# Reordering the hand-over between a layer norm and the next projection in an fp32 transformer kernel

## The reference

```python
def hybrid_layer(x, ...):
    proj = einsum('bsd,de->bse', x, w_in)        # 1024 -> 4864 columns
    ...                                          # pooling, window attention, gated conv
    mix = einsum('bsd,de->bse', merged, w_o)
    x = layer_norm(ALPHA * x + mix, ln1_g, ln1_b)
    up = causal_dwconv(einsum('bsd,df->bsf', x, w_up), ffn_conv_w)
    a, b = split(up, 2)
    ffn = einsum('bsf,fd->bsd', silu(a) * b, w_down)
    return layer_norm(ALPHA * x + ffn, ln2_g, ln2_b)
```

## Time and profile before

| what | value |
|---|---|
| time, median of 3 runs | 2985.54 us (2983.82 to 2987.83) |
| time of the profiled execution | 2989.49 us |
| its span, first to last instruction | 2987.5 us |
| mean granted TensorE clock | 0.994 of full speed |
| busy: PE / ACT / DVE / POOL | 2912.5 / 1591.6 / 1060.3 / 411.8 us |

### The profile page before, as it was taken

One profiled execution on the slowest core, in us unless ns is written; L12 is line 12 of the kernel. 1 busy time (PEld: TensorE's weight loads), 2 busy tenths in 40 slices (PEclk: granted clock), 3 DMA queues, 4 the chain that ended last, 5 costly groups with the idle time before them and its releaser, 6 DMA issues.

```text
span 2987.5 us, 35252 instructions
## 1 busy us (share of the span) xinstructions
PE 2912.5 (97%) x13262; PEld 2376.9 (80%) x13262; DVE 1060.3 (35%) x2146; ACT 1591.6 (53%) x2305; POOL 411.8 (14%) x477
## 2 busy tenths in 40 slices
PE   8999999999999999999998999999999899999997
PEld 6889888888887568888887887888877788788885
DVE  4534436321123764121226114422253611632234
ACT  6655656554445755444455445545554544554455
POOL 1111111111111001111110111111111011111111
PEclk9999999999999999999999999999999999999998
DMA  8676767688987328888883887787877299788876
GB/s 240 147 149 136 161 138 154 144 198 194 194 191 169 71 43 188 196 193 194 195 192 70 188 192 168 183 197 192 191 167 171 58 201 193 156 195 191 201 184 158
DMA packets 138148, 503.65 MB, mean 169 GB/s; under 512 B 15472, under 2 KB 15728, under 8 KB 137872
## 3 DMA queue, kind: packets, MB, share of 16 engines
q0 software_dynamic: 68016, 248.22, 47.2%
q1 hardware_dynamic: 69120, 251.69, 27.7%
q10 hardware_dynamic: 864, 1.72, 0.2%
HBM read 499.46 MB, written 2.10 MB: 168 GB/s over the span
## 4 chain that ended last, share of the span: by engine, by line
PE 91%; DVE 3%; ACT 2%; issue 2%; DMA 1%; DVEq 1%; ACTq 0%; POOLq 0%; POOL 0%; SPq 0%
PE ps L971 74%; PE ps L989 5%; PE ps L1342 3%; PE ps L1063 1%; DMA wl<-weights 1%; PE ps L1120 1%; PE ps L1264 1%; PE ps L1283 1%; PE ps L1265 1%; DVE arena L2086 1%; PE ps L1103 0%; PE ps L1209 0%; ACT wl L430 0%; PE ps L1272 0%; PE ps L1234 0%
## 5 line engine op out<-in xcount | busy, mean ns | idle before, releaser
L426 ACT ACTIVATE wh<-raw 128x1024 fp32r<-128x1024 f32 (+1 forms) x470 | 495.0, 1053 | 1079.8 <-PE ps L971 999.8
L971 PE MATMUL ps<-HH,wh 128*128 128x512 f32 x2304 | 905.8, 393 | 13.6 <-DVE HL L1975 5.7
L971 PE MATMUL ps<-HH,wl 128*128 128x512 f32 x2304 | 897.7, 390 | 0.0
L971 PE MATMUL ps<-HL,wh 128*128 128x512 f32 x2304 | 897.6, 390 | 0.0
L410 POOL DMA_DIRECT2D wl<-weights x470 | 409.9, 872 | 2570.7 <-ACT wl L430 2566.0
L971 PEld LDWEIGHTS ps<-HH,wh 128*128 128x128 f32 x2304 | 433.3, 188 | 110.8 <-issue 21.8
L971 PEld LDWEIGHTS ps<-HL,wh 128*128 128x128 f32 x2304 | 433.4, 188 | 91.8 <-issue 3.1
L971 PEld LDWEIGHTS ps<-HH,wl 128*128 128x128 f32 x2304 | 433.1, 188 | 90.8
L430 ACT ACTIVATE wl<-raw 128x1024 fp32r<-128x1024 f32 (+1 forms) x470 | 488.4, 1039 | 0.0
L971 PE MATMUL ps<-MH,wh 128*128 128x512 f32 x1056 | 411.9, 390 | 1.8 <-issue 0.8
L971 PE MATMUL ps<-MH,wl 128*128 128x512 f32 x1056 | 410.9, 389 | 0.0
(11 more groups left out here) (277 smaller groups left out, 2756.4 us busy)
## 6 DMA issues: line engine op xcount, KB each, us to landing
raw<-weights SPq DMA_DIRECT2D x472, 512.0 KB, 5.4
wl<-weights POOLq DMA_DIRECT2D x470, 512.0 KB, 7.8
XT<-x SPq DMA_DIRECT2D x4, 512.0 KB, 6.6
out<-XT SPq DMA_DIRECT2D x4, 512.0 KB, 2.7
arena<-tables POOLq DMA_DIRECT2D x1, 1024.0 KB, 12.2
arena<-table_h ACTq DMA_DIRECT2D x1, 640.0 KB, 6.0
arena<-swaps_a POOLq DMA_DIRECT2D x1, 576.0 KB, 8.0
lpar<-layers ACTq DMA_DIRECT2D x2, 218.0 KB, 2.7
```

The source lines that it names most:

```text
L426: act_f(wh[:, n, 0:w], raw[:, n, 0:w], ACT.Copy)
L971: op = mm(bank(g, t), w[:, slot, at:at + P], x[:, first + kt, :], start=(kt == 0 and w is wh and x is xh), stop=(kt == n_k - 1 and w is wl))
```

## The change

Three edits. (1) ACT's program at the head of a layer: the wait for `h_ready` and the DMA of the layer's numbers stand behind the four slabs of the first set instead of ahead of them. (2) DVE's loop in the norm: `low(t)` stands right behind `scaled(t)` and `off(t+3)` of its own tile, and a drain stands behind each tile. The order becomes s0 o3 l0, s1 o4 l1, s2 o5 l2, s3 o6 l3, s4 o7 l4, s5 l5, s6 l6, s7 l7. (3) TensorE's program for a set that follows a norm: step kt = 0 first waits for the high part of tile 0 alone (`split_hi`), does the 8 matmuls that read it, then waits for the low part and does the other 4. The same matmuls are issued, in another order.

```diff
             for layer in turns(c, DEPTH2, H_LAYER):
                 hl = c.take("hl")
+                g, last = set_of(4)
                 act.wait_ge(h_ready, hl.value(1))
                 act.dma_start(lpar[:, :], layer_in[layer]).then_inc(layer_load, 16)
-                g, last = set_of(4)
                 wait_used(act, last)
...
-            def features(nslab, xh, xl, ready, first=0, n_tiles=4, width=512, per_slab=2, between=None, at=1, inside=None):
+            def features(nslab, xh, xl, ready, first=0, n_tiles=4, width=512, per_slab=2, between=None, at=1, inside=None,
+                         high_ready=None):
...
                 def body(g, slot, k, kt):
+                    if kt == 0 and high_ready is not None:
+                        high_ready()
+                        for t in range(n_tiles):
+                            for w in (wh, wl):
+                                mm(bank(g, t), w[:, slot, t * P:(t + 1) * P], xh[:, first, :], start=w is wh, stop=False)
+                        ready(0)
+                        for t in range(n_tiles):
+                            mm(bank(g, t), wh[:, slot, t * P:(t + 1) * P], xl[:, first, :], start=False, stop=False)
+                        return None
                     ready(kt)
...
-            def up_part(first, sets, ready):
+            def high_of(s):
+                return lambda: pe.wait_ge(split_hi, s.value(1))
+
+            def up_part(first, sets, ready, high_ready=None):
                 s = c.at["split"]
                 for k in range(sets):
-                    features(4, HH, HL, ready)
+                    features(4, HH, HL, ready, high_ready=None if k else high_ready)
...
-                features(4, HH, HL, split_ready(c.at["split"] + (-KT)))
+                entered = c.at["split"] + (-KT)
+                features(4, HH, HL, split_ready(entered), high_ready=high_of(entered))
...
-                    up_part(first, sets, nothing if first else split_ready(s1))
+                    up_part(first, sets, nothing if first else split_ready(s1), None if first else high_of(s1))
...
                 for t in range(KT):
                     scaled(t)
-                    if t and not end:
-                        low(t - 1)
                     if t + 3 < KT:
                         op = off(t + 3)
                         if t + 4 == KT:
                             op.then_inc(acc_free[gl.mod(2)], FREE)
-                        dve.drain()
+                    if not end:
+                        low(t)
+                    dve.drain()
                 if end:
                     return
-                low(KT - 1)
```

## The result

The changed kernel is slower: 2996.31 us median of 6 runs (2995.28 to 2999.36), against 2985.38 us for the kernel before (6 runs, 2983.82 to 2988.89). The ratio is 1.0036, 95% interval 1.0023 to 1.0049, so 0.2 to 0.5% slower. The medians are 10.9 us apart; the forecast was 2998 us, 12.8 above the median it started from. The profiled execution took 2998.16 us, its span 2996.4 us (before 2987.5).

A forecast was written before the change was run, and what follows sets the result against it. PE, busy 97% of the span, was taken as the bound, so only its gaps count. Late second sets 8.1, layer's DMA 0, last norm 0.3, clock 4.4: +12.8 on 2985.54 gives 2998 us, range 2990 to 3003.

The forecast's parts named there:

- The step on which everything rests: At all three norms PE's second set starts by when ACT finishes its eighth tile, 11.42 to 12.03 us from slab start.
- Edit 2's tile: DVE's new order makes each tile a serial round trip of 2.37 us; eighth high part ends after 18.1 us.
- Restarts behind the first norms: PE's second sets behind both layers' first norms start 4.13 and 3.8 to 4.15 us later, 8.1 us in sum.
- Edit 3: PE's first set starts 1.3 us earlier, waits 0.4 at step 1; lost at the second set's gap, counted nothing.
- Edit 1: Layer 1's head: slab starts 0.4 us earlier, the layer's DMA may cost 0.8; taken as 0, between -0.4 and +0.4.
- crowded as feared: Layer 1's head: the layer's 218 KB DMA runs during the fifth slab's `wl` transfer, taking 0.8 us at that rate.
- The last norm: Drains behind tiles 5 and 6 add 2 x 0.16 = 0.3 us on the path to the output.
- The clock: Two new 5.9 us gaps behind the first norms halve PE's clock; 2.2 us each, 4.4 together, bounds 0 and 5.4.
- the rival in which the clock holds: Clock stays up behind the new gaps at the second sets: +8.4 us, 2994 us; chance 0.20.

The follow-up runs named there:

- edit2: Kernel before with only DVE's new loop (each low part right behind its tile's scaling, a drain behind each tile): 3001.88 us.
- edit23: Changed kernel with ACT's wait for `h_ready` and the layer's DMA put back ahead of the first set's slabs: 3001.43 us.
- busy5: Changed kernel plus 5 calls of a matmul on constants ahead of the second set behind each of the three norms: 2991.61 us.
- edit3: Kernel before with only PE's first contraction step changed, to begin with the 8 matmuls that read the high part: 2982.72 us.
- edit13: Changed kernel with DVE's old loop, so low parts come in the old order: 2979.05 us.
- edit1: Kernel before with only the first set's four slabs moved ahead of the wait for `h_ready` and the layer's DMA: 2980.91 us.

## Why the prediction was right

**The step on which everything rests** was that PE's second set starts when ACT's fifth slab allows it. It held: with the slab behind a late eighth tile (the changed kernel, `edit2`, `edit23`, `busy5`) the restart came 2.7 to 3.6 us later at the first norm of layer 0 and 3.3 to 4.1 us later at that of layer 1, except 1.5 us in `edit2`, where the transfer was quick; of six restarts that followed a PE start 1.3 to 1.7 us earlier with the old loop (`edit3`, `edit13`) five stayed within 0.3 us of those without it (the sixth had a quick transfer), and taking the slab out from behind the tiles removed the gaps. The label "issue" for the gaps of 0.88 and 0.78 us hid a wait for a `wl` transfer.

**Edit 2's tile.** 2.37 us forecast, 2.39 measured; 18.1 us from the first scaling to the end of the eighth high part, 18.22 to 18.24 measured. Restarts behind the first norms: 3.8 to 4.15 and 4.13 us later forecast, 3.48 and 4.12 measured. In layer 0 the transfer went a little quicker: 11.60 us from ACT's start to PE's restart against 12.03.

**Edit 3.** The first matmul was forecast 1.67 us behind the first scaling and came at 1.65 to 1.66. The wait ahead of step 1 was forecast at 0.4 us and is 0.3 (step 1 starts at 1864.70, where 1861.62 + 2.75 = 1864.37 would be free). The start was counted at nothing. `edit3` (1.8 us faster, interval up to 1.0001) and `edit23` (0.5 us below `edit2`) are not told from nothing, though a quick transfer can let some of it through.

**Edit 1.** This is the term that was mis-sized. It was 0, between -0.4 and +0.4; the restart came 0.86 us sooner, outside these bounds. The ACT part was right (the slab starts 0.28 us sooner). The transfer was not crowded as feared: 8.48 us from POOL's issue to PE's restart, 9.05 before, though the layer's DMA was issued 4.7 us ahead of that restart. The transfer that suffered was the layer's own DMA (last section). The Trainium skill's rule (Trainium Kernel Development and Optimization, Key Constraints), that all issuers' DMAs share the same engines and interleave, agrees with the latter; it does not say which of two transfers pays. Alone, edit 1 is worth 3.6 us: the prediction had the ACT part of it, 4.4 us at that place, eaten by edit 2's late tiles.

**The last norm.** 0.3 us forecast; from its first scaling to the end of the span it is 18.34 us now and 17.88 before, 0.46 more, of which 0.36 lie in the last three scalings (2.44 us against 2.08).

**The clock.** 2.2 us forecast at each new gap, 1.9 and 2.2 measured in the profiled execution: both new gaps paid, at less than the 2.7 of the old one. `busy5` puts the whole price of the three gaps' clock at 4.7 us net. That the clock would fall was read from two gaps of the trace; the 2.2 was a choice between 0 and 2.7, so its closeness is partly luck. The time alone would not have settled it: 10.9 us lies between the 8.4 of the rival in which the clock holds and the 12.8 forecast. The clock in the windows and `busy5` decide.

**The sum.** By the terms as the traces have them, 3.5 + 4.1 - 0.9 + 0.5 + 4.1 for the clock is 11.3, where 12.8 was forecast and the medians lie 10.9 apart. Of the 1.5 us between forecast and terms, 0.9 are edit 1's. The two spans lie only 8.9 us apart. The rest is in stretches that the change does not touch: the one ahead of the first norm was 1.1 us shorter in the profiled execution of the changed kernel, 1.6 and 0.5 us of later waits were absent, and 0.8 us the other way are not assigned. I have no cause for these. Late restarts do not explain the absent waits, as `edit2` and `edit1` showed, and single executions of one kernel differ by 4 to 10 us in any case.

## What to carry to other kernels

Before a producer loop is reordered to hand its first tile over sooner, look at what its helper engine does behind the last tile: here the consumer's next stall hung on that, and an earlier start only lengthened the stall. An order that runs one tile behind is what hides a round trip between two engines; putting each step right behind its own tile made the loop about 30% longer. And a short gap booked as "issue" at the end of a set is worth following back, since moving one slab's preparation into idle time took 20 us off the changed kernel and left it 9 us faster than the one before.

## What the runs showed of the hardware

The same DMA of 218 KB landed 2.4 us after its issue when the DMA engines were idle (before, layer 1's head) and 9.0 us after it among the slabs' transfers (changed kernel). This is from the issues of the two traces, with columns as in the page's last part:

```profile
lpar<-layers ACTq DMA_DIRECT2D x1, 218.0 KB, 2.4
```

```profile
lpar<-layers ACTq DMA_DIRECT2D x1, 218.0 KB, 9.0
```

The length of a gap alone did not decide whether the clock fell. In the kernel before, it stayed at full behind a gap of 2.79 us, and 8 matmuls took 3.70 us. In the changed kernel the same 8 matmuls, behind a gap of 2.78 us at the same place, took 5.32 us, and the clock was at half. The change does not touch this stretch:

```profile
972.21 5.32 PE L1246 MATMUL ps<-arena,cst 128*128 128x512 f32 x8 [2.78 <-DVE arena L1784]
```

```profile
972.21:975.00 2.79, 2.79 (x4) 1.24 (x5) 2.59 (x5) 0.00 (x0) 0.00 (x0) 0.50 0.00 0
```

The prediction had read it off one gap of each length (0.78, 2.79, 3.51 and 4.83 us). The fall need not come with the restart either. In `edit2` it came half a microsecond behind the restart from a gap of 2.85 us, as the matmuls' durations and the windows show:

```profile
2633.96 0.47 PE L971 MATMUL ps<-HH,wh 128*128 128x512 f32 x1 [2.85 <-issue]
2634.27 0.43 PE L971 MATMUL ps<-HL,wh 128*128 128x512 f32 x1
2634.50 0.63 PE L971 MATMUL ps<-HH,wl 128*128 128x512 f32 x1
```

```profile
2634.00:2635.00 1.00, 1.00 (x4) 0.82 (x5) 1.00 (x2) 1.00 (x3) 0.87 (x1) 0.74 1.11 266
2635.00:2636.00 1.00, 1.00 (x4) 0.81 (x3) 1.00 (x3) 0.98 (x2) 0.00 (x0) 0.50 0.98 258
```
